# Four FFN layers, four base addresses: moving a kernel's split weights and block sums by 64 to 192 bytes

## The chip, the cores and the metric

The kernel runs on one NeuronCore of a Trainium2 chip, as one program. The metric is device microseconds of that core; lower is better. The time before is 1921.73 us, the median of 3 runs (1921.44 to 1924.72).

## The reference, cut to what matters

Two layers, each a feed-forward network (FFN), a mixer, and another FFN, on 512 tokens of width 1024 in float32. There are four FFNs, and only they matter here:

```
def swiglu(x, w_gate, w_up, w_down):
    return (jax.nn.silu(x @ w_gate) * (x @ w_up)) @ w_down

h = rms_norm(x, ffn1_norm[i])
x = x + 0.5 * swiglu(h, ffn1_w_gate[i], ffn1_w_up[i], ffn1_w_down[i])
# ... a mixer (recurrence, convolution, attention) ...
h = rms_norm(x, ffn2_norm[i])
x = x + 0.5 * swiglu(h, ffn2_w_gate[i], ffn2_w_up[i], ffn2_w_down[i])
```

The hidden width is 2816, that is 22 tiles of 128.

## The kernel before, in words

**Precision.** Every float32 operand is split in two fp32r parts, hi (written by ACT) and lo (the rest, written by DVE). A product is three matmuls on TensorE (PE): hi times hi, lo of the moving operand times hi of the weights, hi of the moving operand times lo of the weights. `product` (lines 797 to 799) and `gu_product` (lines 861 to 863) issue these three. Each matmul has its own load of 128x128 weights, which shows under PEld and runs beside the matmul before it.

**A hidden tile.** Tokens are handled transposed: 128 rows of the width on the partitions, tokens along the free dimension. The first two tiles of each layer are "plain" (`plain_tile`): gate and up, eight blocks of the width, 2 x 8 x 3 = 48 matmuls of 512 columns. The other 20 ("hidden" tiles, `hidden_tile`) use a scheme with seven products in place of eight on halves of the tokens: per product 4 pairs of blocks x 3 = 12 matmuls of 256 columns. The seven weight pieces of a tile (gate, up, and sums of them) lie in `gw_hi` and `gw_lo`. Pieces 0, 1, 5 and 6 are multiplied with `xs_hi`/`xs_lo`, the split input; pieces 2, 3 and 4 with `xu_hi`/`xu_lo`, the split block sums of the input, which are made once a layer. A full tile issues pieces 0, 1, 2, then 6 of the tile before, then 3, 4 and 5: 84 matmuls. All wait on counting semaphores (`gw_lo_done`, `copy_done`, `prod_done`); ACT's next split of a piece (`gw_high`) waits for the product that read the piece before.

**The rest.** After 6, 14 and 22 tiles, down units multiply the hidden activations `a_hi`/`a_lo` with streamed weights `w_hi`/`w_lo`, in matmuls of 512 columns. SP issues the loads of `gu` (the raw gate and up weights) and `raw` in a written-out order; POOL adds two of the sums by DMA. The order on every engine is written by hand.

**Addresses.** `sb` places tiles one after another on every partition, in multiples of 32 bytes, or at a byte that it is told. The bases in the program before are:

| tile | base | base modulo 256 |
|---|---|---|
| xs_hi, xs_lo | 17536, 33920 | 128 |
| w_hi, w_lo | 66688, 74880 | 128 |
| a_hi, a_lo | 83072, 99456 | 128 |
| t0, t1, t2 | 121920 and on | 64 |
| gu | 153280 | 192 |
| gw_hi, gw_lo | 175808, 190144 | 192 |
| xu_hi, xu_lo | 204480, 216768 | 192 |

Every block, piece, pair and token half inside these FFN tiles is a multiple of 512 bytes away from its base, so each FFN matmul reads its moving operand and its weights at these residues.

Of the kernel before, what the change touches and what calls it, by code (L numbers as in the profile page):

```python
# [7 lines left out]
F32 = mybir.dt.float32  # L8
F32R = mybir.dt.float32r
# [5 lines left out]
P = 128  # L15
# [172 lines left out]
def build(nc, xt_in, gu_stream, w_stream, vec_in, bd_in, relb_in, onehot_in, ident_in, out):  # L188
# [3 lines left out]
    with ExitStack() as ctx:  # L192
        top = [(nc.sbuf_base + 31) // 32 * 32]

        def sb(name, shape, dt=F32, at=None):

            size = int(np.prod(shape[1:])) * 4
            if at is None:
                at, top[0] = top[0], top[0] + (size + 31) // 32 * 32
            return nc.alloc_sbuf_tensor_at(name, shape, dt, offset=at)  # L200
# [47 lines left out]
        head_sel = sb("head_sel", [P, 2])  # L248
        stage = top[0]
        gu = sb("gu", [P, 11, PIECE])  # L250
        gw_hi = sb("gw_hi", [P, 7, PIECE], F32R)
        gw_lo = sb("gw_lo", [P, 7, PIECE], F32R)
        xu_hi = sb("xu_hi", [P, PAIRS, 3 * TH], F32R)
        xu_lo = sb("xu_lo", [P, PAIRS, 3 * TH], F32R)
        ffn_top = top[0]

        top[0] = stage
        q_hi = sb("q_hi", [P, 2, T], F32R)
# [310 lines left out]
        def plain_bank(r, which):  # L569
            return (ps_s, ps_t)[r][:, which, :]  # L570
# [223 lines left out]
        def _(pe):  # L794
# [57 lines left out]
                start_unit(n)  # L852
                blocks(s, range(KT), of_x(1), of_x(0)).then_inc(unit_done, 1)

            def gu_product(ps, piece, hi, lo, first, wait=None):

                for j in range(PAIRS):
                    if wait:
                        wait(j)
                    w = slice(j * P, (j + 1) * P)  # L860
                    pe.matmul(ps, gw_hi[:, piece, w], hi(j), start=first and j == 0, stop=False, skip_group_check=True)  # L861
                    pe.matmul(ps, gw_hi[:, piece, w], lo(j), start=False, stop=False, skip_group_check=True)  # L862
                    mm = pe.matmul(ps, gw_lo[:, piece, w], hi(j), start=False, stop=j == PAIRS - 1, skip_group_check=True)  # L863
                mm.then_inc(prod_done, 1)

            def of_u(d, part):
# [1 line left out]
                w = slice(part * TH, (part + 1) * TH)  # L868
                return lambda j: xs_hi[:, 2 * j + d, w], lambda j: xs_lo[:, 2 * j + d, w]

            def of_xu(part):
                w = slice(part * TH, (part + 1) * TH)
                return lambda j: xu_hi[:, j, w], lambda j: xu_lo[:, j, w]

            def square_sum(i):
                pe.wait_ge(const_done, 2)
# [9 lines left out]
            def plain_part(f, j, which, k):  # L886

                piece, w = PLAIN_PIECES[j][2 * (k % 2) + which], slice(k // 2 * P, k // 2 * P + P)
                if k == 0:
                    pe.wait_ge(gw_lo_done, 1 + which if f == 0 else split_count(f, 0))  # L890
                if k == 1:
                    pe.wait_ge(gw_lo_done, split_count(f, 1))
                return product(plain_bank(f % 2, which), gw_hi[:, piece, w], gw_lo[:, piece, w], xs_hi[:, k, :], xs_lo[:, k, :],
                               not plain_started[which], k == KT - 1)

            plain_started = [False, False]
# [34 lines left out]
            def hidden_tile(f, j, i):  # L931

                r, first, more, n = f % 2, j == PLAIN, pended(j), BLOCK_NO[f]
                operands = 4 * FFN_NO[i]

                def landed(sem):
                    return (lambda k: pe.wait_ge(sem, operands + k + 1)) if first else None

                def a12_u2():
                    pe.wait_ge(gw_lo_done, split_count(f, 3))  # L940
                    gu_product(block_bank(r, 0), 5, *of_u(1, 0), True)

                pe.wait_ge(gw_lo_done, split_count(f, 0))
                if n:
                    pe.wait_ge(copy_done, 3 * n)
                gu_product(chain, 0, *of_u(0, 0), True)
                if plain(f - 2):
                    pe.wait_ge(hidden_done, f - 1)
                else:
                    pe.wait_ge(gate_done, 2 * (f - 2) + 1)  # L950
                gu_product(block_bank(r, 2), 1, *of_u(0, 1), True, landed(ua_done))
                pe.wait_ge(gw_lo_done, split_count(f, 1))
                pe.wait_ge(copy_done, 3 * n + 1)
                gu_product(chain, 2, *of_xu(1), False, landed(uc_done))
                if not more:
                    a12_u2()
                elif not plain(f - 1):
                    gate_right(f - 1)
                pe.wait_ge(gw_lo_done, split_count(f, 2))
                if first:  # L960
                    gu_product(block_bank(r, 1), 4, *of_xu(2), False)
                pe.wait_ge(copy_done, 3 * n + 2)
                gu_product(chain, 3, *of_xu(0), False)
                if not first:
                    gu_product(block_bank(r, 1), 4, *of_xu(2), False)
                if more:
                    a12_u2()

            def gate_right(f):

                pe.wait_ge(gw_lo_done, split_count(f, 4))
                pe.wait_ge(up_done, BLOCK_NO[f] + 1)
                gu_product(block_bank(f % 2, 2), 6, *of_u(1, 1), False)

            def down_part(i, u, ks):

# [327 lines left out]
        def _(act):  # L1304
# [48 lines left out]

            def block_x_hi(i, j):
                act.wait_ge(u4_done, PAIRS * FFN_NO[i] + j + 1)
                act.activation(xu_hi[:, j, :].rearrange("p (h t) -> p h t", t=TH), scr[j][:, 3:6, :], ACT.Copy).then_inc(uc_hi_done, 1)

            def right_x_hi(i, j):

# [7 lines left out]
            def plain_high(f, k):  # L1367

                j, r = f % FT, f % 2
                w, src = plain_split(k, j, r)  # L1370
                act.wait_ge(gu_landed[r], landed_count(f))
                if (j, k) == (1, 1):
                    act.wait_ge(prod_done, prod_count(f - 1, "odd"))
                elif f - j:
                    act.wait_ge(prod_done, prod_count(f - j - 1, 3))
                act.activation(gw_hi[:, w, :], src, ACT.Copy, scale=-1.0 if k else 1.0).then_inc(gw_hi_done, 1)

            def norm_std(i):
                act.wait_ge(ssq_done, i + 1)
# [3 lines left out]
            def gw_high(f, k):  # L1383

                r, n = f % 2, BLOCK_NO[f]
                w, src = gu_split(k, r)
                if k == 0:
                    act.wait_ge(gu_landed[r], landed_count(f))
                    act.wait_ge(s1_landed, 16 * (n + 1))
                elif k == 2:  # L1390
                    act.wait_ge(s3_landed, 16 * (n + 1))
                elif k != 3:
                    act.wait_ge(sum_done, 2 * n + (1 if k == 1 else 2))
                if plain(f - 1):
                    act.wait_ge(prod_done, prod_count(f - (2 if k < 2 else 1), "even" if k == 2 else "odd"))
                else:
                    act.wait_ge(prod_done, prod_count(f - 1, (5, 6, 7 if plain(f - 2) else 4, 2, 3)[k]))
                act.activation(gw_hi[:, w, :], src, ACT.Copy).then_inc(gw_hi_done, 1)  # L1398

            def chain_copy(f, p, out):  # L1400
                act.wait_ge(prod_done, prod_count(f, p))
# [429 lines left out]
            act.wait_ge(vec_landed, 16)  # L1831
            act.wait_ge(s1_loaded[0], 16)
            for part in range(2):
                act.activation(gw_hi[:, part, :], gu[:, part, :], ACT.Copy).then_inc(gw_hi_done, 1)
                if part == 0:
                    act.wait_ge(x_landed[0], 16)
                    split_x(0, 0)
# [16 lines left out]
        def _(dve):  # L1854
# [942 lines left out]
```

## Time and profile before

| what | before |
|---|---|
| median of 3 runs | 1921.73 us |
| span of the profiled execution (its own time, first to last instruction) | 1922.5 us |
| PE busy | 1887.3 us (98%) |
| DVE busy | 1462.5 us (76%) |
| ACT busy | 1020.9 us (53%) |
| matmuls | 11902 |

A busy PE in this profile is not a PE at its peak: matmuls overlap, each is shown with a latency, and what one costs is the distance from its start to the start of the next.

### The profile page before, as it was taken

The numbers are of one execution on the slowest core, as the hardware profiler recorded it, in microseconds if no ns is written. First come the engines' busy times: TensorE is split into PE (matmuls) and PEld (weight loads), VectorE is DVE, ScalarE is ACT, GpSimd is POOL, SyncE is SP. The second block draws the span as 40 slices with busy tenths as digits, with TensorE's granted clock in tenths as the row PEclk, the third lists the DMA queues.
The fourth block names the chain that finished last, engine by engine and source line by source line (L and its number), as shares of the span: only waits on it lengthen the run. The fifth ranks groups of instructions, "written<-read, shape, count | busy, mean of one in ns | idle before, by whom it ended". The sixth has DMA issues, their size and how long they took to land.

```text
span 1922.5 us, 31441 instructions
## 1 busy us (share of the span) xinstructions
PE 1887.3 (98%) x11902; PEld 1674.8 (87%) x11902; DVE 1462.5 (76%) x2330; ACT 1020.9 (53%) x1640; POOL 193.0 (10%) x251
## 2 busy tenths in 40 slices
PE   7999999999999999999999999999999999999999
PEld 6899799888878899898889989887778779898997
DVE  8878487667779778597887949756988878687684
ACT  7546154477776455264644626454455766364451
POOL 1311010000001111010110101011111001011010
PEclk9999999999999999999999999999999999999999
DMA  7666862321126655462466646166765376566441
GB/s 240 169 171 182 131 188 61 110 77 57 65 102 173 170 151 152 149 175 97 136 167 165 166 132 181 50 152 161 171 148 133 85 202 171 157 168 168 133 115 66
DMA packets 94662, 271.18 MB, mean 141 GB/s; under 512 B 10568, under 2 KB 10824, under 8 KB 94512
## 3 DMA queue, kind: packets, MB, share of 16 engines
q1 hardware_dynamic: 63456, 201.22, 31.7%
q0 software_dynamic: 29232, 64.50, 19.4%
q10 hardware_dynamic: 1824, 3.44, 1.0%
q8 instruction: 95, 1.56, 0.3%
q14 instruction: 55, 0.45, 0.1%
HBM read 223.07 MB, written 2.28 MB: 117 GB/s over the span
## 4 chain that ended last, share of the span: by engine, by line
PE 85%; DVE 8%; ACT 3%; issue 2%; DMA 1%; ACTq 0%; DVEq 0%
PE ps_unit L797 12%; PE ps_unit L798 12%; PE ps_unit L799 12%; PE ps_y L861 6%; PE ps_y L863 6%; PE ps_y L862 6%; PE ps_s L861 4%; PE ps_s L863 4%; PE ps_s L862 4%; PE ps_t L861 4%; PE ps_t L863 3%; PE ps_t L862 3%; PE ps_s L797 1%; PE ps_s L798 1%; PE ps_s L799 1%
## 5 line engine op out<-in xcount | busy, mean ns | idle before, releaser
L1398 ACT ACTIVATE gw_hi<-gu 128x512 fp32r<-128x512 f32 (+1 forms) x400 | 318.9, 799 | 151.0 <-PE ps_s L863 67.5
L1932 DVE TENSOR_TENSOR gw_lo<-gu,gw_hi 128x512 fp32r<-128x512 f32 (+1 forms) x400 | 354.8, 901 | 49.0 <-ACT gw_hi L1398 36.7
L797 PE MATMUL ps_unit<-a_hi,w_hi 128*128 128x512 f32 x892 | 352.8, 395 | 9.2 <-DVE w_lo L1860 6.5
L798 PE MATMUL ps_unit<-a_lo,w_hi 128*128 128x512 f32 x892 | 349.1, 391 | 0.0
L799 PE MATMUL ps_unit<-a_hi,w_lo 128*128 128x512 f32 x845 | 330.1, 391 | 0.0
L1333 ACT ACTIVATE w_hi<-raw 128x1024 fp32r<-128x1024 f32 (+1 forms) x125 | 125.2, 1003 | 314.0 <-PE ps_unit L799 296.3
L797 PEld LDWEIGHTS ps_unit<-a_hi,w_hi 128*128 128x128 f32 x892 | 168.4, 189 | 48.8 <-DVE w_lo L1860 9.4
L2065 DVE TENSOR_TENSOR t<-ps_unit,half 128x512 f32<-128x512 f32 x96 | 66.4, 691 | 172.4 <-PE ps_unit L799 171.8
L798 PEld LDWEIGHTS ps_unit<-a_lo,w_hi 128*128 128x128 f32 x892 | 168.4, 189 | 33.2
L799 PEld LDWEIGHTS ps_unit<-a_hi,w_lo 128*128 128x128 f32 x845 | 159.5, 189 | 34.1
L861 PE MATMUL ps_y<-xu_hi,gw_hi 128*128 128x256 f32 x640 | 180.3, 282 | 0.3 <-ACT sqb L1402 0.3
L863 PE MATMUL ps_y<-xu_hi,gw_lo 128*128 128x256 f32 x640 | 180.3, 282 | 0.0
L862 PE MATMUL ps_y<-xu_lo,gw_hi 128*128 128x256 f32 x640 | 179.4, 280 | 0.0
L1860 DVE TENSOR_TENSOR w_lo<-raw,w_hi 128x1024 fp32r<-128x1024 f32 (+1 forms) x125 | 143.9, 1152 | 22.9 <-ACT w_hi L1333 22.9
L742 POOL DMA_DIRECT2D gu<-gu_stream_dram x80 | 74.5, 931 | 728.7 <-DMA gu<-gu_stream_dram 722.0
L797 PE MATMUL ps_unit<-xs_hi,w_hi 128*128 128x512 f32 x360 | 145.8, 405 | 0.0
L798 PE MATMUL ps_unit<-xs_lo,w_hi 128*128 128x512 f32 x360 | 140.3, 390 | 0.0
L861 PE MATMUL ps_t<-xs_hi,gw_hi 128*128 128x256 f32 x480 | 134.3, 280 | 2.1 <-DVE t L1994 2.1
L861 PE MATMUL ps_s<-xs_hi,gw_hi 128*128 128x256 f32 x480 | 133.5, 278 | 0.0
L862 PE MATMUL ps_s<-xs_lo,gw_hi 128*128 128x256 f32 x480 | 133.2, 277 | 0.0
L862 PE MATMUL ps_t<-xs_lo,gw_hi 128*128 128x256 f32 x480 | 133.1, 277 | 0.0
L863 PE MATMUL ps_t<-xs_hi,gw_lo 128*128 128x256 f32 x480 | 132.9, 277 | 0.0
(322 smaller groups left out, 4666.9 us busy)
## 6 DMA issues: line engine op xcount, KB each, us to landing
gu<-gu_stream_dram SPq DMA_DIRECT2D x176, 512.0 KB, 5.2
raw<-w_stream_dram SPq DMA_DIRECT2D x136, 512.0 KB, 3.3
gu<-gu_stream_dram SPq DMA_DIRECT2D x80, 256.0 KB, 3.0
gu<-gu_stream_dram POOLq DMA_DIRECT2D x80, 256.0 KB, 4.5
gu<-gu POOLq DMA_DIRECT2D x80, 256.0 KB, 3.3
w_lo<-raw POOLq DMA_DIRECT2D x28, 512.0 KB, 5.1
raw<-w_stream_dram SPq DMA_DIRECT2D x32, 384.0 KB, 3.5
w_lo_3rd<-raw POOLq DMA_DIRECT2D x15, 512.0 KB, 5.2
```

The lines of the kernel that those rows point to most:

```text
L742: pool.dma_start(gu[:, 8 + r, :], gu_stream[f, 1][:, 1, :], accum_op=ALU.add).then_inc(s1_landed, 16)
L797: pe.matmul(ps, lhs_hi, rhs_hi, start=first, stop=False)
L798: pe.matmul(ps, lhs_hi, rhs_lo, start=False, stop=False)
L799: return pe.matmul(ps, lhs_lo, rhs_hi, start=False, stop=last)
L861: pe.matmul(ps, gw_hi[:, piece, w], hi(j), start=first and j == 0, stop=False, skip_group_check=True)
L862: pe.matmul(ps, gw_hi[:, piece, w], lo(j), start=False, stop=False, skip_group_check=True)
L863: mm = pe.matmul(ps, gw_lo[:, piece, w], hi(j), start=False, stop=j == PAIRS - 1, skip_group_check=True)
L1333: act.activation(w_hi[:, s, 0:width(n)], raw[:, slot, 0:width(n)], ACT.Copy).then_inc(w_hi_done, 1)
L1398: act.activation(gw_hi[:, w, :], src, ACT.Copy).then_inc(gw_hi_done, 1)
L1860: dve.tensor_tensor(w_lo[:, s, w], raw[:, slot, w], w_hi[:, s, w].bitcast(F32), ALU.subtract).then_inc(w_lo_done, 1)
L1932: dve.tensor_tensor(gw_lo[:, w, :], src, gw_hi[:, w, :].bitcast(F32), ALU.subtract).then_inc(gw_lo_done, 1)
L2065: dve.tensor_tensor(t0[:, :], ps_unit[:, s, :], half[:, :], ALU.mult).then_inc(unit_read, 1)
```

## The change

In each of the four FFN layers (counted 0 to 3) `gw_hi`, `gw_lo`, `xu_hi` and `xu_lo` become tensors of their own, at bases that are shifted by a number of bytes. All instructions, waits, loads and their order stay. The residues modulo 256 that follow are:

| layer | gw before | gw after | xu before | xu after | xs (not moved) |
|---|---|---|---|---|---|
| 0 | 192 | 192 | 192 | 128 | 128 |
| 1 | 192 | 0 | 192 | 192 | 128 |
| 2 | 192 | 128 | 192 | 192 | 128 |
| 3 | 192 | 64 | 192 | 192 | 128 |

```
+GW_SHIFT = (0, 64, 192, 128)
+XU_SHIFT = (192, 256, 256, 256)
...
-        gw_hi = sb("gw_hi", [P, 7, PIECE], F32R)
-        gw_lo = sb("gw_lo", [P, 7, PIECE], F32R)
-        xu_hi = sb("xu_hi", [P, PAIRS, 3 * TH], F32R)
-        xu_lo = sb("xu_lo", [P, PAIRS, 3 * TH], F32R)
-        ffn_top = top[0]
+        gw_at, xu_at = top[0], top[0] + 2 * 7 * PIECE * 4
+        gw_hi = [sb(f"gw_hi{n}", [P, 7, PIECE], F32R, at=gw_at + GW_SHIFT[n]) for n in range(4)]
+        gw_lo = [sb(f"gw_lo{n}", [P, 7, PIECE], F32R, at=gw_at + GW_SHIFT[n] + 7 * PIECE * 4) for n in range(4)]
+        xu_hi = [sb(f"xu_hi{n}", [P, PAIRS, 3 * TH], F32R, at=xu_at + XU_SHIFT[n]) for n in range(4)]
+        xu_lo = [sb(f"xu_lo{n}", [P, PAIRS, 3 * TH], F32R, at=xu_at + XU_SHIFT[n] + PAIRS * 3 * TH * 4) for n in range(4)]
+        ffn_top = xu_at + max(XU_SHIFT) + 2 * PAIRS * 3 * TH * 4
...
-                    pe.matmul(ps, gw_hi[:, piece, w], hi(j), start=first and j == 0, stop=False, skip_group_check=True)
+                    pe.matmul(ps, gw_hi[f // FT][:, piece, w], hi(j), start=first and j == 0, stop=False, skip_group_check=True)
...
-                return lambda j: xu_hi[:, j, w], lambda j: xu_lo[:, j, w]
+                return lambda j: xu_hi[f // FT][:, j, w], lambda j: xu_lo[f // FT][:, j, w]
```

Every other place that names one of the four tiles takes the layer's own in the same way.

## Rows read from the trace of the kernel before

**Rows 1.** The page: span, busy time of each engine (share, instructions).
```profile
span 1922.5 us, 31441 instructions
...
PE 1887.3 (98%) x11902; PEld 1674.8 (87%) x11902; DVE 1462.5 (76%) x2330; ACT 1020.9 (53%) x1640; POOL 193.0 (10%) x251
```

**Rows 2.** Windows, four tiles each: length; PE, PEld, DVE, ACT, POOL; clock, DMA share, GB/s.
```profile
130.53:169.57 39.04, 39.04 (x338) 39.04 (x337) 35.30 (x49) 24.34 (x42) 6.43 (x8) 1.00 0.72 188
697.89:736.93 39.04, 39.04 (x339) 39.04 (x337) 35.30 (x49) 24.30 (x42) 7.01 (x8) 1.00 0.72 190
1039.54:1078.58 39.04, 39.04 (x339) 39.04 (x338) 35.29 (x49) 24.29 (x42) 6.99 (x8) 1.00 0.74 190
...
1814.75:1853.79 39.04, 39.04 (x339) 39.04 (x337) 35.32 (x49) 24.32 (x42) 6.54 (x8) 1.00 0.74 188
```

**Rows 3.** Timeline of PE in two tiles of layer 0: start, length, matmul.
```profile
150.05 0.28 PE L861 MATMUL ps_y<-xs_hi,gw_hi 128*128 128x256 f32 x1
...
151.41 0.28 PE L861 MATMUL ps_s<-xs_hi,gw_hi 128*128 128x256 f32 x1
...
156.99 0.28 PE L861 MATMUL ps_s<-xu_hi,gw_hi 128*128 128x256 f32 x1
...
158.43 0.29 PE L861 MATMUL ps_s<-xs_hi,gw_hi 128*128 128x256 f32 x1
...
162.53 0.28 PE L861 MATMUL ps_y<-xu_hi,gw_hi 128*128 128x256 f32 x1
```

**Rows 4.** Groups by form, matmuls with gw weights: count, busy us, mean ns.
```profile
L861 PE MATMUL ps_y<-xu_hi,gw_hi 128*128 128x256 f32 x640 | 180.3, 282 | 0.3 <-ACT sqb L1402 0.3
...
L861 PE MATMUL ps_t<-xs_hi,gw_hi 128*128 128x256 f32 x480 | 134.3, 280 | 2.1 <-DVE t L1994 2.1
L861 PE MATMUL ps_s<-xs_hi,gw_hi 128*128 128x256 f32 x480 | 133.5, 278 | 0.0
...
L861 PE MATMUL ps_y<-xs_hi,gw_hi 128*128 128x256 f32 x320 | 88.7, 277 | 0.0
...
L861 PE MATMUL ps_s<-xu_hi,gw_hi 128*128 128x256 f32 x160 | 45.3, 283 | 0.0
...
L861 PE MATMUL ps_t<-xu_hi,gw_hi 128*128 128x256 f32 x160 | 45.3, 283 | 0.0
...
L797 PE MATMUL ps_t<-xs_hi,gw_hi 128*128 128x512 f32 x64 | 27.2, 425 | 0.0
```

**Rows 5.** Timeline of PE: a plain tile of layer 2, then an output unit.
```profile
941.54 0.39 PE L799 MATMUL ps_t<-xs_hi,gw_lo 128*128 128x512 f32 x1
...
943.41 0.39 PE L798 MATMUL ps_t<-xs_lo,gw_hi 128*128 128x512 f32 x1
...
547.64 0.39 PE L797 MATMUL ps_unit<-a_hi,w_hi 128*128 128x512 f32 x1
...
549.90 0.39 PE L798 MATMUL ps_unit<-a_lo,w_hi 128*128 128x512 f32 x1
```

**Rows 6.** Timeline of DVE in the first of those tiles, layer 0.
```profile
159.31 0.69 DVE L1932 TENSOR_TENSOR gw_lo<-gu,gw_hi 128x512 fp32r<-128x512 f32 x1
```

**Rows 7.** Groups by form, whole span: DVE and ACT with other operand addresses.
```profile
L1932 DVE TENSOR_TENSOR gw_lo<-gu,gw_hi 128x512 fp32r<-128x512 f32 x240 | 164.9, 687 | 24.9 <-ACT gw_hi L1398 18.6
...
L1398 ACT ACTIVATE gw_hi<-gu 128x512 fp32r<-128x512 f32 x240 | 151.0, 629 | 107.3 <-PE ps_s L863 42.0 <-DVE gu L1952 35.8 <-PE ps_t L863 29.5
...
L2003 DVE TENSOR_TENSOR a_lo<-t,a_hi 128x512 fp32r<-128x512 f32 x88 | 60.4, 687 | 6.8 <-ACT a_hi L1413 5.6
...
L1413 ACT ACTIVATE a_hi<-t 128x512 fp32r<-128x512 f32 x88 | 55.7, 633 | 9.5 <-DVE t L1999 8.4 <-DVE t L1972 1.0
```

**Rows 8.** Layer 0 around 200 us: timelines of ACT and PE, then a window.
```profile
195.81 7.78 ACTq L1663 DMA_DIRECT2D bias_t<-skew  x16
...
206.06 0.79 PE L797 MATMUL ps_unit<-a_hi,w_hi 128*128 128x512 f32 x1 [3.66 <-DVE w_lo L1860]
...
205.34:212.16 6.82, 6.09 (x14) 4.79 (x15) 3.79 (x5) 0.36 (x1) 0.00 (x0) 0.50 0.89 110
```

More of the change, by code:

```diff
@@ L853, in x_unit, with gu_product @@
                 blocks(s, range(KT), of_x(1), of_x(0)).then_inc(unit_done, 1)
-            def gu_product(ps, piece, hi, lo, first, wait=None):
+            def gu_product(f, ps, piece, hi, lo, first, wait=None):
                 for j in range(PAIRS):
@@ L860, in gu_product @@
                     w = slice(j * P, (j + 1) * P)
-                    pe.matmul(ps, gw_hi[:, piece, w], hi(j), start=first and j == 0, stop=False, skip_group_check=True)
-                    pe.matmul(ps, gw_hi[:, piece, w], lo(j), start=False, stop=False, skip_group_check=True)
-                    mm = pe.matmul(ps, gw_lo[:, piece, w], hi(j), start=False, stop=j == PAIRS - 1, skip_group_check=True)
+                    pe.matmul(ps, gw_hi[f // FT][:, piece, w], hi(j), start=first and j == 0, stop=False, skip_group_check=True)
+                    pe.matmul(ps, gw_hi[f // FT][:, piece, w], lo(j), start=False, stop=False, skip_group_check=True)
+                    mm = pe.matmul(ps, gw_lo[f // FT][:, piece, w], hi(j), start=False, stop=j == PAIRS - 1, skip_group_check=True)
                 mm.then_inc(prod_done, 1)
@@ L869, in of_u, with of_xu @@
                 return lambda j: xs_hi[:, 2 * j + d, w], lambda j: xs_lo[:, 2 * j + d, w]
-            def of_xu(part):
+            def of_xu(f, part):
                 w = slice(part * TH, (part + 1) * TH)
-                return lambda j: xu_hi[:, j, w], lambda j: xu_lo[:, j, w]
+                return lambda j: xu_hi[f // FT][:, j, w], lambda j: xu_lo[f // FT][:, j, w]
             def square_sum(i):
@@ L892, in plain_part @@
                     pe.wait_ge(gw_lo_done, split_count(f, 1))
-                return product(plain_bank(f % 2, which), gw_hi[:, piece, w], gw_lo[:, piece, w], xs_hi[:, k, :], xs_lo[:, k, :],
+                return product(plain_bank(f % 2, which), gw_hi[f // FT][:, piece, w], gw_lo[f // FT][:, piece, w], xs_hi[:, k, :], xs_lo[:, k, :],
                                not plain_started[which], k == KT - 1)
@@ L940, in a12_u2 @@
                     pe.wait_ge(gw_lo_done, split_count(f, 3))
-                    gu_product(block_bank(r, 0), 5, *of_u(1, 0), True)
+                    gu_product(f, block_bank(r, 0), 5, *of_u(1, 0), True)
                 pe.wait_ge(gw_lo_done, split_count(f, 0))
@@ L945, in hidden_tile @@
                     pe.wait_ge(copy_done, 3 * n)
-                gu_product(chain, 0, *of_u(0, 0), True)
+                gu_product(f, chain, 0, *of_u(0, 0), True)
                 if plain(f - 2):
@@ L950, in hidden_tile @@
                     pe.wait_ge(gate_done, 2 * (f - 2) + 1)
-                gu_product(block_bank(r, 2), 1, *of_u(0, 1), True, landed(ua_done))
+                gu_product(f, block_bank(r, 2), 1, *of_u(0, 1), True, landed(ua_done))
                 pe.wait_ge(gw_lo_done, split_count(f, 1))
                 pe.wait_ge(copy_done, 3 * n + 1)
-                gu_product(chain, 2, *of_xu(1), False, landed(uc_done))
+                gu_product(f, chain, 2, *of_xu(f, 1), False, landed(uc_done))
                 if not more:
@@ L960, in hidden_tile @@
                 if first:
-                    gu_product(block_bank(r, 1), 4, *of_xu(2), False)
+                    gu_product(f, block_bank(r, 1), 4, *of_xu(f, 2), False)
                 pe.wait_ge(copy_done, 3 * n + 2)
-                gu_product(chain, 3, *of_xu(0), False)
+                gu_product(f, chain, 3, *of_xu(f, 0), False)
                 if not first:
-                    gu_product(block_bank(r, 1), 4, *of_xu(2), False)
+                    gu_product(f, block_bank(r, 1), 4, *of_xu(f, 2), False)
                 if more:
@@ L972, in gate_right @@
                 pe.wait_ge(up_done, BLOCK_NO[f] + 1)
-                gu_product(block_bank(f % 2, 2), 6, *of_u(1, 1), False)
+                gu_product(f, block_bank(f % 2, 2), 6, *of_u(1, 1), False)
             def down_part(i, u, ks):
@@ L1355, in block_x_hi @@
                 act.wait_ge(u4_done, PAIRS * FFN_NO[i] + j + 1)
-                act.activation(xu_hi[:, j, :].rearrange("p (h t) -> p h t", t=TH), scr[j][:, 3:6, :], ACT.Copy).then_inc(uc_hi_done, 1)
+                act.activation(xu_hi[FFN_NO[i]][:, j, :].rearrange("p (h t) -> p h t", t=TH), scr[j][:, 3:6, :], ACT.Copy).then_inc(uc_hi_done, 1)
             def right_x_hi(i, j):
@@ L1375, in plain_high @@
                     act.wait_ge(prod_done, prod_count(f - j - 1, 3))
-                act.activation(gw_hi[:, w, :], src, ACT.Copy, scale=-1.0 if k else 1.0).then_inc(gw_hi_done, 1)
+                act.activation(gw_hi[f // FT][:, w, :], src, ACT.Copy, scale=-1.0 if k else 1.0).then_inc(gw_hi_done, 1)
             def norm_std(i):
@@ L1397, in gw_high @@
                     act.wait_ge(prod_done, prod_count(f - 1, (5, 6, 7 if plain(f - 2) else 4, 2, 3)[k]))
-                act.activation(gw_hi[:, w, :], src, ACT.Copy).then_inc(gw_hi_done, 1)
+                act.activation(gw_hi[f // FT][:, w, :], src, ACT.Copy).then_inc(gw_hi_done, 1)
             def chain_copy(f, p, out):
@@ L1833, in _ @@
             for part in range(2):
-                act.activation(gw_hi[:, part, :], gu[:, part, :], ACT.Copy).then_inc(gw_hi_done, 1)
+                act.activation(gw_hi[0][:, part, :], gu[:, part, :], ACT.Copy).then_inc(gw_hi_done, 1)
                 if part == 0:
@@ L1894, in block_x_lo @@
                 dve.wait_ge(uc_hi_done, PAIRS * FFN_NO[i] + j + 1)
-                dve.tensor_tensor(xu_lo[:, j, :].rearrange("p (h t) -> p h t", t=TH), scr[j][:, 3:6, :],
-                                  xu_hi[:, j, :].rearrange("p (h t) -> p h t", t=TH).bitcast(F32), ALU.subtract).then_inc(uc_done, 1)
+                dve.tensor_tensor(xu_lo[FFN_NO[i]][:, j, :].rearrange("p (h t) -> p h t", t=TH), scr[j][:, 3:6, :],
+                                  xu_hi[FFN_NO[i]][:, j, :].rearrange("p (h t) -> p h t", t=TH).bitcast(F32), ALU.subtract).then_inc(uc_done, 1)
             def right_x_lo(i, j):
@@ L1931, in gw_low @@
                 dve.wait_ge(gw_hi_done, split_count(f, k))
-                dve.tensor_tensor(gw_lo[:, w, :], src, gw_hi[:, w, :].bitcast(F32), ALU.subtract).then_inc(gw_lo_done, 1)
+                dve.tensor_tensor(gw_lo[f // FT][:, w, :], src, gw_hi[f // FT][:, w, :].bitcast(F32), ALU.subtract).then_inc(gw_lo_done, 1)
             def plain_low(f, k):
@@ L1938, in plain_low @@
                 if k:
-                    dve.scalar_tensor_tensor(gw_lo[:, w, :], src, -1.0, gw_hi[:, w, :].bitcast(F32), ALU.mult, ALU.subtract).then_inc(gw_lo_done, 1)
+                    dve.scalar_tensor_tensor(gw_lo[f // FT][:, w, :], src, -1.0, gw_hi[f // FT][:, w, :].bitcast(F32), ALU.mult, ALU.subtract).then_inc(gw_lo_done, 1)
                 else:
-                    dve.tensor_tensor(gw_lo[:, w, :], src, gw_hi[:, w, :].bitcast(F32), ALU.subtract).then_inc(gw_lo_done, 1)
+                    dve.tensor_tensor(gw_lo[f // FT][:, w, :], src, gw_hi[f // FT][:, w, :].bitcast(F32), ALU.subtract).then_inc(gw_lo_done, 1)
             def second_sum(f):
@@ L2658, in _ @@
                 dve.wait_ge(gw_hi_done, part + 1)
-                dve.tensor_tensor(gw_lo[:, part, :], gu[:, part, :], gw_hi[:, part, :].bitcast(F32), ALU.subtract).then_inc(gw_lo_done, 1)
+                dve.tensor_tensor(gw_lo[0][:, part, :], gu[:, part, :], gw_hi[0][:, part, :].bitcast(F32), ALU.subtract).then_inc(gw_lo_done, 1)
                 if part == 0:
```

## The prediction

> **What bounds the kernel now.** I read the page first: PE is busy for 1887.3 of 1922.5 us, 98%, and DVE, the next, for 76% [rows 1]. Then I cut out steady stretches of each FFN layer. Four hidden tiles take 39.04 us in layer 0 and exactly as long in layers 1, 2 and 3, with PE busy throughout at the full clock and DVE for 35.3 us [rows 2]. So a hidden tile costs 39.04 / 4 = 9.76 us, PE paces it, and it does not depend on what else a layer does. Last I read the starts of single matmuls, because no instruction, wait or transfer is added or removed: only what one matmul costs can change.
>
> There the reader is to see that equal matmuls don't cost the same. Piece 0, moving operand xs, has 12 matmuls of 256 columns from 150.05 to 151.41: 0.1133 us each. Piece 4, moving operand xu, has 12 of the same shape, with weights from the same tile, from 156.99 to 158.43: 0.1200 us each [rows 3]. The lengths tell the same, 277 to 280 ns with xs against 282 or 283 with xu [rows 4]. These two prices make the whole tile: 48 xs matmuls x 0.1133 + 36 xu matmuls x 0.1200 = 5.44 + 4.32 = 9.76 us, the measured period [rows 2]. Nothing is left for waits, and the extra is 0.0067 us for each xu matmul, 36 x 0.0067 = 0.24 us a tile.
>
> **What could make the difference.** I write d for the base of the moving operand minus that of the weights, modulo 256. From the table of bases, xs with gw has d = 192, and xu with gw has d = 0. Matmuls of 512 columns give two more points. In a plain tile (xs with gw, d = 192) eight starts take 943.41 - 941.54 = 1.87 us, 0.2337 each; in an output unit (a with w, d = 0) ten take 549.90 - 547.64 = 2.26 us, 0.226 each [rows 5]. So d = 0 is the slow one at 256 columns and the fast one at 512:
>
> | columns | d = 192 | d = 0 |
> |---|---|---|
> | 256 | 0.1133 us | 0.1200 us |
> | 512 | 0.2337 us | 0.226 us |
>
> In units of 0.0067 us, the difference, these are 17 and 18 units, then 35 and 34. The odd numbers of units stand with d = 192, an odd number of 64 bytes, the even ones with d = 0, an even number. The simplest rule with all four points: a matmul takes at least 17 units (256 columns) or 34 (512), and one more where the parity of d / 64 asks for it. I call it the parity rule. It makes d = 64 behave as 192 and d = 128 as 0. No row shows d = 64 or d = 128 in an FFN matmul, so both prices are open between 0 and 0.0067 us of extra, by the nearest rows.
>
> The Trainium skill speaks against any effect: "SBUF — State Buffer", section "SBUF: two separate sides", gives TensorE two independent read ports, one for the moving operand and one for the weights, and says that TensorE waits for nobody. By that rule the four residues would cost the same and the time would stay. The trace disagrees, with 0.1133 against 0.1200 us [rows 3].
>
> **The change part by part.** Counts first. Each of the three matmuls of a product appears 640 + 160 + 160 = 960 times with xu and 480 + 480 + 320 = 1280 times with xs [rows 4]; over three lines and four layers that is 720 xu and 960 xs matmuls of 256 columns a layer. The plain tiles have 96 of 512 columns a layer (64 in one of six such groups). One unit on all of them is 720 x 0.0067 = 4.8 us, 960 x 0.0067 = 6.4 us and 96 x 0.0067 = 0.64 us.
>
> - Layer 0: xu goes from d = 0 to 128 - 192 = 192, the residues that xs and gw already have in this trace. The price is read, not guessed: minus 4.8 us. xs stays.
> - Layer 1 (gw at 0): xu gets d = 192, minus 4.8 us, with both residues moved by 64. xs gets d = 128: by parity plus 6.4 us, and the plain tiles lose their extra, minus 0.64 us. Sum plus 0.96 us.
> - Layer 2 (gw at 128): xu gets d = 64, by parity minus 4.8 us. xs gets d = 0, the slow distance at 256 columns and the fast one at 512: plus 6.4 minus 0.64 us. Sum plus 0.96 us.
> - Layer 3 (gw at 64): xu gets d = 128, by parity as slow as now. xs gets d = 64, by parity as fast as now. Sum 0.
> - ACT and DVE write and read the moved tiles. DVE takes 687 ns for 128x512 whether all lie at residue 192 or at 64 and 128; ACT takes 629 and 633 ns [rows 7]. I take 0; the bound is 4 ns x 400 splits = 1.6 us of ACT time, which PE's queue covers (next point).
> - Does a faster PE only wait later? DVE needs 35.3 / 4 = 8.8 us a tile [rows 2], and a tile with all matmuls at 0.1133 takes 84 x 0.1133 = 9.52 us, so DVE still fits. Of the splits that PE waits for, the one at 159.31 ends at 160.00 and its product (piece 2 of the next tile) starts at 162.53, 2.5 us later [rows 3, 6]. A gain of 0.24 us a tile lies within that. So tile time goes to the end in full.
> - Layer 0 has one stall, 3.66 us at 202 to 206 us, because ACT issues 16 DMAs for 7.78 us ahead of a weight split, and after it PE runs for 6.8 us at half clock (1.2 GHz) [rows 8]. The issue follows an ACT instruction of the last tile, so the stall moves with PE and eats nothing. Whether the clock falls again is open: 6.8 us at half speed cost 3.4 us, and I keep that as a bound on both sides.
>
> Sum by the parity rule: -4.8 + 0.96 + 0.96 + 0 = -2.9 us. On the profiled execution 1922.5 becomes 1919.6; its span is 0.8 us over the median of the runs, so the median becomes 1918.8 us.
>
> **The rivals.** With x and y for the extra of d = 64 and d = 128 at 256 columns, in units, the sum is: layer 0 -4.8; layer 1 -4.8 + 6.4 y; layer 2 -4.8 + 6.4 - 0.64 + 4.8 x; layer 3 -4.8 + 6.4 x + 4.8 y. Together -13.4 + 11.2 (x + y), and up to 1.3 us less by the plain tiles of layers 1 and 3. Parity is x = 0, y = 1.
>
> - Only equal residues cost (x = y = 0): minus 13.4, 1908.3 us, or 1907.0 with the plain tiles. For it: the one slow case at 256 columns is d = 0. Against it: at 512 columns d = 0 is the fast one, so equality alone doesn't cost.
> - Only d = 192 is a good fit at 256 columns (x = y = 1): the xs products of layers 1 to 3 pay 6.4 us each, only layers 0 and 1 win with xu, plus 9.0 us, 1930.7 us: slower. It decides from x + y = 1.2 on. For it: one good distance is all that the trace shows. Against it: the good distance differs between 256 and 512 columns, so it is no single one.
> - The moving operand's address alone counts (192 slow, 128 fast): only layer 0 wins, minus 4.8 us, 1916.9 us. Against it: 512-column matmuls with moving residue 128 cost 0.226 or 0.2337 us by what the weights' tile is [rows 5].
> - The address is not the cause, something else in xu is: no change, 1921.7 us. Against it: the moving data differ in nothing else that a matmul sees.
>
> **How the numbers follow.** Parity 0.48, equal residues only 0.2, only d = 192 0.1, moving operand alone 0.08, no effect 0.06, values of x and y in between 0.08. The likeliest gives 1918.8 us; its own range is 1915.4 to 1922.2, by the clock's 3.4 us. The range for all is 1906.5 to 1925.0: it takes in equal residues with the plain tiles and leaves out the slow rival. About 0.2%, 3.8 us, is what a measurement of this kernel can tell from no change. Parity's 2.9 us is below that, and I give it 0.1 of its 0.48 above the bound and 0.01 on the slow side. Faster: 0.1 + 0.2 + 0.05 + 0.03 = 0.38. Slower: 0.1 + 0.01 + 0.05 of the mixed and clock cases = 0.16. The same: 0.46.
>
> **What would show it.** In layer 0 four hidden tiles should take 4 x 9.52 = 38.1 us, with xu matmuls 0.1133 us apart; this is the surest step. In layers 1 and 2 four tiles should take 4 x (36 x 0.1133 + 48 x 0.12) = 39.4 us, with the slow matmuls now those of xs and the plain tiles' at 0.227; in layer 3 39.04 as now. If layer 1's xs matmuls stay at 0.1133 us, y is 0 and the time falls under 1915; if layer 3's rise to 0.12, x is 1 and the kernel is slower. The prediction is wrong at its root if xu in layer 0 stays at 0.12.

## The result, and the profile after

The changed kernel takes 1932.02 us (median of 3 runs, 1927.64 to 1932.78), 1.0044 of the time before, with a 95% interval of 1.0031 to 1.0057: slower by 0.44%, where 1918.8 us and most likely "the same" were forecast.

The page of the kernel after, the lines that answer to [rows 1]:

```profile
span 1931.0 us, 31441 instructions
...
PE 1893.5 (98%) x11902; PEld 1682.4 (87%) x11902; DVE 1462.9 (76%) x2330; ACT 1020.7 (53%) x1640; POOL 193.3 (10%) x251
```

The same instructions, DVE and ACT unchanged to 0.4 us, PE 6.2 us busier, the span 8.5 us longer. Where it went, by layer: the timeline of PE, the first FFN matmul of layers 1, 2 and 3, before and then after:

```profile
582.27 0.40 PE L797 MATMUL ps_s<-xs_hi,gw_hi 128*128 128x512 f32 x1
...
923.93 0.40 PE L797 MATMUL ps_s<-xs_hi,gw_hi 128*128 128x512 f32 x1
...
1576.59 0.40 PE L797 MATMUL ps_s<-xs_hi,gw_hi 128*128 128x512 f32 x1
```
```profile
583.04 0.40 PE L800 MATMUL ps_s<-xs_hi,gw_hi 128*128 128x512 f32 x1
...
925.82 0.39 PE L800 MATMUL ps_s<-xs_hi,gw_hi 128*128 128x512 f32 x1
...
1583.05 0.39 PE L800 MATMUL ps_s<-xs_hi,gw_hi 128*128 128x512 f32 x1
```

Four hidden tiles of each layer after, windows with the columns of [rows 2]:

```profile
130.31:169.88 39.57, 39.57 (x338) 39.57 (x337) 35.29 (x49) 24.32 (x42) 6.34 (x9) 1.00 0.72 187
698.97:738.25 39.28, 39.28 (x339) 39.28 (x338) 35.32 (x49) 24.33 (x41) 6.59 (x8) 1.00 0.70 186
1042.10:1082.15 40.05, 40.05 (x339) 40.05 (x337) 35.32 (x49) 24.28 (x42) 6.95 (x8) 1.00 0.71 186
1812.27:1851.95 39.68, 39.68 (x338) 39.68 (x337) 35.15 (x48) 24.39 (x41) 6.16 (x8) 1.00 0.66 175
```

Behind the down groups every layer's tile is longer than the 39.04 / 4 = 9.76 us of [rows 2], with PE at its full clock (1.00) and busy throughout. The differences between layer starts, with the mixers in them, and 1931.0 - 1583.05 for the last, give the account:

| layer | a tile behind the down groups, after | predicted | layer's change, measured | predicted |
|---|---|---|---|---|
| 0 | 9.89 us | 9.52 us | +0.77 us | -4.8 us |
| 1 | 9.82 us | 9.84 us | +1.12 us | +0.96 us |
| 2 | 10.01 us | 9.84 us | +4.57 us | +0.96 us |
| 3 | 9.92 us | 9.76 us | +2.04 us | 0 |

The column measured adds up to the 8.5 us. Layer 0, the step called the surest, is the one most wrong. Its timeline of PE shows why: the end of the tile ahead of the first down group, the products behind it, and the tile of [rows 3]:

```profile
74.51 0.28 PE L864 MATMUL ps_t<-xs_hi,gw_hi 128*128 128x256 f32 x1
...
75.87 0.40 PE L800 MATMUL ps_unit<-a_hi,w_hi 128*128 128x512 f32 x1
...
78.22 0.36 PE L864 MATMUL ps_t<-xs_hi,gw_hi 128*128 128x256 f32 x1 [0.80 <-DVE t L1997]
78.41 0.28 PE L865 MATMUL ps_t<-xs_lo,gw_hi 128*128 128x256 f32 x1
...
79.59 0.28 PE L866 MATMUL ps_t<-xs_hi,gw_lo 128*128 128x256 f32 x1
...
150.10 0.28 PE L864 MATMUL ps_y<-xs_hi,gw_hi 128*128 128x256 f32 x1
...
151.51 0.28 PE L864 MATMUL ps_s<-xs_hi,gw_hi 128*128 128x256 f32 x1
```

Up to 75.87 us twelve matmuls take 1.36 us, 0.1133 each, as in [rows 3]. From 78.41 on ten take 1.18 us, and at 150.10 twelve take 1.41 us: 0.118 us each, with xs and gw at the same addresses as before. So d = 192 has two paces, 0.1133 us (9.52 us a tile) and about 0.1178 us (9.89 / 84). The four tiles ahead of the first down group got the first, the sixteen behind it the second.

The trace of the kernel before has both paces too. Its timeline of PE in layer 0, behind the first down group: the first two xs products, then the third matmul of the xs product that follows the first xu product, and the start of the next product:

```profile
112.25 0.28 PE L861 MATMUL ps_y<-xs_hi,gw_hi 128*128 128x256 f32 x1
...
113.66 0.28 PE L861 MATMUL ps_s<-xs_hi,gw_hi 128*128 128x256 f32 x1
...
116.76 0.28 PE L863 MATMUL ps_s<-xs_hi,gw_lo 128*128 128x256 f32 x1
...
117.89 0.28 PE L861 MATMUL ps_y<-xu_hi,gw_hi 128*128 128x256 f32 x1
```

Right behind the down group twelve xs matmuls take 1.41 us, 0.1178 each; behind the first xu product ten take 1.13 us, 0.113 each. All eight down groups of that trace are followed by this change.

In layer 2 both even and odd distances appear (timeline of PE):

```profile
946.00 0.39 PE L800 MATMUL ps_t<-xs_hi,gw_hi 128*128 128x512 f32 x1
...
947.81 0.39 PE L802 MATMUL ps_t<-xs_hi,gw_lo 128*128 128x512 f32 x1
...
1052.11 0.28 PE L864 MATMUL ps_y<-xs_hi,gw_hi 128*128 128x256 f32 x1
...
1053.55 0.28 PE L864 MATMUL ps_t<-xs_hi,gw_hi 128*128 128x256 f32 x1
...
1059.27 0.28 PE L864 MATMUL ps_t<-xu_hi,gw_hi 128*128 128x256 f32 x1
...
1060.68 0.29 PE L864 MATMUL ps_t<-xs_hi,gw_hi 128*128 128x256 f32 x1
```

xs (d = 0) takes 1.44 / 12 = 0.1200 us, and the plain tile at d = 0 takes 1.81 / 8 = 0.226 us, both as predicted; xu (d = 64) takes 1.41 / 12 = 0.1175 us, where 0.1133 was forecast.

### The profile page after: what moved, and what is told of

Read it like the earlier page. It is cut to its first block, busy times and chain, and to the rows that moved or that the text cites. A ratio compares the mean times of both kernels' runs of the same rounds, so it can differ in the third digit from the quotient of the medians.

```text
span 1931.0 us, 31441 instructions
## 1 busy us (share of the span) xinstructions
PE 1893.5 (98%) x11902; PEld 1682.4 (87%) x11902; DVE 1462.9 (76%) x2330; ACT 1020.7 (53%) x1640; POOL 193.3 (10%) x251
## 3 DMA queue, kind: packets, MB, share of 16 engines
q0 software_dynamic: 29232, 64.50, 19.4%
## 4 chain that ended last, share of the span: by engine, by line
PE 81%; DVE 10%; ACT 3%; issue 3%; DMA 2%; ACTq 0%; DVEq 0%; POOL 0%; POOLq 0%
PE ps_unit L800 12%; PE ps_unit L802 12%; PE ps_unit L801 12%; PE ps_y L864 5%; PE ps_y L866 5%; PE ps_y L865 5%; PE ps_s L866 4%; PE ps_s L864 4%; PE ps_s L865 4%; PE ps_t L864 4%; PE ps_t L866 3%; PE ps_t L865 3%; PE ps_s L800 1%; DMA raw<-w_stream_dram 1%; DVE cv L2456 1%
## 5 line engine op out<-in xcount | busy, mean ns | idle before, releaser
L866 PE MATMUL ps_s<-xs_hi,gw_lo 128*128 128x256 f32 x480 | 135.0, 281 | 0.0
```

The costliest lines, as they stand in the source:

```text
L866: mm = pe.matmul(ps, gw_lo[f // FT][:, piece, w], hi(j), start=False, stop=j == PAIRS - 1, skip_group_check=True)
```

## The experiments

**The theory of two paces:** at an odd distance (64 or 192 bytes) a matmul of 256 columns runs steadily at 0.1133 or at 0.1178 us, and what PE did just before decides which. In the kernel before, the slow xu stretches (d = 0) in every tile brought the xs stretches to the quick pace, so giving xu d = 192 too takes that away. Its rival: d = 192 costs 0.1133 us by itself, and something else in layer 0 costs the rest. Letters in the expectations are those of each expectation.

**d = 192 for both operands in all four layers.** The edit, against the changed kernel:

```
-GW_SHIFT = (0, 64, 192, 128)
-XU_SHIFT = (192, 256, 256, 256)
+GW_SHIFT = (0, 0, 0, 0)
+XU_SHIFT = (192, 192, 192, 192)
```

> gw stays at residue 192 in all four layers and xu goes to 128 in all four, so that every 256-column matmul with gw weights has d = 192. Theory A, memory of the pace: at d = 192 there are two steady paces, 0.1133 and 0.1178 us, and the stretch of matmuls before decides which one a run of equal matmuls falls into and keeps. Each layer then starts at 0.1133 us (hidden tile 9.52 us) and changes to 0.1178 us (9.89 us) at its first down group, as layer 0 of the changed kernel did: about +0.8 us a layer, 1925 us. Rival B, something in layer 0 alone (its start, its transfers) slowed it there: layers 1 to 3 keep 9.52 us, -4.8 us each, about 1908 us.

Measured 1926.27 us, 1.0021 of before (1.0012 to 1.0031). Windows of layer 1, two tiles ahead of the first down group and four behind it:

```profile
612.83:631.87 19.04, 19.04 (x171) 19.04 (x169) 18.13 (x26) 12.80 (x22) 3.50 (x4) 1.00 0.76 196
695.39:734.97 39.58, 39.58 (x339) 39.58 (x337) 35.30 (x49) 24.31 (x42) 6.17 (x8) 1.00 0.71 187
```

9.52 us a tile ahead, 9.89 behind, in all four layers. The rival falls. Here xs and gw lie where they lay before; only xu moved, and the xs products behind the down groups lost their 0.1133 us. Their price depended on their neighbours.

**Other distances.** The edit, against the changed kernel:

```
-GW_SHIFT = (0, 64, 192, 128)
-XU_SHIFT = (192, 256, 256, 256)
+GW_SHIFT = (128, 192, 64, 0)
+XU_SHIFT = (192, 192, 192, 64)
```

> One distance for xs and xu in each of the first three layers: d = 64 in layer 0, d = 0 in layer 1, d = 128 in layer 2; in layer 3 d = 192 for xs and 64 for xu. Theory A with the parity rule for the paces that exist: layer 1 has one pace, 0.1200 us, 10.08 us a tile; layers 0 and 3 have 9.52 us before the first down group and 9.89 us after it; layer 2 about 0.1188 us, as xs of layer 1 in the changed kernel, 9.97 us. The parity rule of the prediction alone: 9.52 us in layers 0 and 3, 10.08 us in layers 1 and 2, throughout.

Measured 1939.08 us, in one run. Windows of layer 1 (d = 0 for both), layer 2 (d = 128 for both: two tiles ahead of the first down group, four behind), layer 3 (xs 192, xu 64: the same two places):

```profile
691.12:731.44 40.32, 40.32 (x338) 40.32 (x337) 35.29 (x48) 24.42 (x41) 6.12 (x7) 1.00 0.64 172
964.06:983.99 19.93, 19.93 (x170) 19.93 (x169) 18.48 (x26) 12.91 (x23) 3.55 (x4) 1.00 0.73 184
1058.26:1098.58 40.32, 40.32 (x338) 40.32 (x337) 35.51 (x49) 24.32 (x41) 6.51 (x8) 1.00 0.70 183
1622.55:1641.93 19.38, 19.38 (x170) 19.38 (x169) 18.45 (x26) 12.93 (x22) 3.52 (x4) 1.00 0.71 190
1695.63:1735.20 39.57, 39.57 (x338) 39.57 (x337) 35.01 (x48) 24.34 (x41) 6.10 (x7) 1.00 0.66 174
```

40.32 / 4 = 10.08 us is 84 x 0.1200: both even distances can cost that all through a tile. Layer 2, forecast at 9.97 throughout, has that ahead of the down group (19.93 / 2) and 10.08 behind it. Layer 3, odd distances only, is at 9.69, where 9.52 was forecast, and then at 9.89. Layer 0 (64 bytes for both) takes 9.52 us for the tile from 66.41 to 75.93 us, ahead of its first down group, and 9.89 behind it. So at 256 columns the even and odd classes are real, and the odd class has the two paces, at 64 bytes as at 192. The paces can also stand side by side: in the tiles of 9.69 us the xs products (192) take 1.36 or 1.37 us and the xu products (64) 1.41.

**Slow matmuls in front of the products, by halving the end of each down group.** The last two blocks of the last down unit of a group are multiplied in halves of 256 columns (12 matmuls at d = 0), once with d = 192 in all layers, once in the kernel before.

```
...
+                pe.matmul(ps, w_hi[:, s, w], hi_x(k)[:, c], start=False, stop=False)
+                pe.matmul(ps, w_hi[:, s, w], lo_x(k)[:, c], start=False, stop=False)
+                mm = pe.matmul(ps, lo[:, w], hi_x(k)[:, c], start=False, stop=last)
...
```

> As e1, and the last two blocks of the last down unit of each group are done in 12 matmuls of 256 columns in place of 6 of 512 (same operands, d = 0, the same sums). Theory A: after 256-column matmuls at d = 0 a d = 192 run falls into the fast pace, as after the xu products of the kernel before; hidden tiles take 9.52 us in all groups, -4.8 us a layer, +0.5 us for the halves, about 1903 us. Rival B, and any theory by which only the addresses of a matmul itself set its cost: within 0.5 us of e1.

> The kernel before with the same halves at the end of each group. Theory A: no change beyond +0.5 us, since each tile's xu products at d = 0 bring the xs products into the fast pace anyway; about 1922 us. A rival by which the halves help of themselves (another wait, a better order): it gains as much as e2 gains on e1.

Measured 1927.86 us (1.0025, 1.0015 to 1.0034) and 1924.54 us (1.0009, 1.0000 to 1.0019). A miss for the first, forecast at about 1903 us: the halves were slow, but the products right behind them stayed at 0.1178, at all eight groups. In the kernel before, the halves gained nothing. Timeline of PE, layer 1, the last halves and the first products, and a window behind them:

```profile
673.92 0.28 PE L995 MATMUL ps_unit<-a_hi,w_hi 128*128 128x256 f32 x1
...
675.35 0.28 PE L865 MATMUL ps_y<-xs_hi,gw_hi 128*128 128x256 f32 x1
```
```profile
693.72:733.29 39.57, 39.57 (x338) 39.57 (x337) 35.29 (x49) 24.30 (x42) 6.12 (x7) 1.00 0.72 187
```

1.43 / 12 = 0.119 us for the halves; 9.89 us a tile. A run of slow matmuls is not enough as such.

Behind one of these eight groups, the second of layer 0, the pace changed later. Timeline of PE at a wait in front of product 2 of the first tile, and a window of four tiles behind it:

```profile
243.74 0.36 PE L865 MATMUL ps_y<-xu_hi,gw_hi 128*128 128x256 f32 x1 [0.29 <-ACT sqb L1426]
```
```profile
250.77:288.85 38.08, 38.08 (x339) 38.08 (x338) 34.97 (x48) 24.33 (x40) 5.27 (x6) 1.00 0.70 187
```

Ahead of this wait of 0.29 us the products run at 0.1178 us, behind it at 0.1133, 9.52 us a tile, for the rest of the group, though no matmul was added there. With d = 192 in all layers and no halves, PE did not wait at this place and stayed at 9.89 us.

**Turns.** A few extra matmuls into the chain's bank just ahead of product 0 of the first hidden tile behind down groups 0 and 1, with d = 192 in all layers; product 0 then starts that sum anew. An offset of 16 elements makes the turn's distance 0.

```
+TURNS = ([(16, 256)] * 1, [(16, 256)] * 2, [(16, 256)] * 4, [(16, 256)] * 9)
...
+                if j > PLAIN and j - 1 in ENDS:
+                    for at, cols in TURNS[f // FT]:
+                        pe.matmul(ps_y[:, 0:cols], gw_hi[f // FT][:, 0, 0:P], xs_hi[:, 0, at:at + cols], start=True, stop=True, skip_group_check=True)
```

> All four layers have the distance 192 bytes for both x operands, as in the run with 192 in all layers, and just before the first gate and up product after down groups 0 and 1 the layers 0, 1, 2 and 3 issue 1, 2, 4 and 9 extra matmuls of 256 columns at distance 0 (their sums land in a bank that is overwritten later). Theory A (a distance-192 product has two steady paces, 0.1133 and 0.1178 us, and the stretch just before decides; a run of slow distance-0 products turns it to the quick one, as each xu stretch did in the kernel before): layer 3 with nine is back at tiles of 9.52 us after each down group instead of 9.89; if one slow product is enough, all layers are, and the kernel takes about 1907 us; with layer 3 alone 1922. Rival B (the quick pace needs slow products in every tile, as the kernel before had): one or two tiles at 9.52 us after each turn, then 9.89, total about 1926. Rival C (what happens before makes no difference, the accumulated work sets it): 9.89 us everywhere after the first group, 1928.

> The same with other turns: layer 0 one extra matmul of 128 columns at distance 192, layer 1 one of 64 columns at distance 192, layers 2 and 3 three and six of 256 columns at distance 0. Theory A: layer 3 (six) goes to tiles of 9.52 us after its down groups, layer 2 lies between one and four of the other run; the short products of layers 0 and 1 only shift the phase: if a phase is what is remembered, one of them turns its layer to 9.52 us as well, else both stay at 9.89. If only layer 3 turns, about 1922 us; if all do, about 1907. Rival C (nothing before makes a difference): 9.89 us everywhere after the first group, 1927.

> As the kernel with 192 in all layers and one turn each, of 256, 192, 32 and 128 columns in layers 0 to 3, all at distance 192. If it is the moment at which a product starts against something periodic that is remembered, a turn of 256 columns, which is one more matmul like those behind it, leaves its layer at 9.89 us after the down groups, and the widths that turn their layer are a matter of length; if any break turns it, all four layers go to 9.52 (about 1905 us). With only the lengths 32 and 128 turning, about 1916.

Measured, one run each: 1915.43, 1908.15 and 1911.29 us (before beside the first two: 1922.01, one run; beside the third: 1922.81). What a tile behind the turn takes:

| turn, per group | layer | tile |
|---|---|---|
| none | all | 9.89 us |
| one of 256 columns, d = 192 | 0 | 9.89 us |
| one of 192 columns, d = 192 | 1 | 9.52 us |
| one of 128 columns, d = 192 | 0 and, in another run, 3 | 9.52 us, in layer 0 behind the first group alone |
| one of 64 columns, d = 192 | 1 | 9.52 us |
| one of 32 columns, d = 192 | 2 | 9.52 us |
| one of 256 columns, d = 0 | 0 | 9.52 us |
| two of 256 columns, d = 0 | 1 | 9.89 us |
| three, four, six, nine, d = 0 | 2, 2, 3, 3 | 9.52 us |

Behind the second group of layer 0 the turn of 128 columns brought the quick pace as well, up to a wait of 0.24 us at 240.06 us; behind that wait the tiles took 9.89 us.

Windows of four tiles: two at d = 0 (layer 1) and nine (layer 3), then 256 columns (layer 0) and 32 columns (layer 2) at d = 192:

```profile
692.73:732.30 39.57, 39.57 (x338) 39.57 (x337) 35.29 (x49) 24.31 (x42) 6.31 (x8) 1.00 0.70 187
1685.67:1723.76 38.09, 38.09 (x339) 38.09 (x338) 35.15 (x49) 24.34 (x41) 7.04 (x8) 1.00 0.75 195
```
```profile
130.03:169.60 39.57, 39.57 (x339) 39.57 (x337) 35.29 (x49) 24.33 (x42) 7.16 (x9) 1.00 0.71 188
1033.58:1071.66 38.08, 38.08 (x338) 38.08 (x337) 35.21 (x49) 24.29 (x41) 6.74 (x8) 1.00 0.75 191
```

One extra matmul changes the price of the next several hundred, so the pace is a state that persists, and neither lengths nor addresses of the products set it alone. One more matmul like those behind it changes nothing, so it is not the extra work or the bank. The rival that slow products are needed in every tile falls.

**The version that gains: 64 columns in every layer, at d = 192 and at the changed kernel's own addresses.**

```
+TURNS = ([(0, 64)],) * 4
```

> Distance 192 bytes for both x operands in all four layers, and one extra matmul of 64 columns before the first gate and up product after down groups 0 and 1 in every layer. Theory A (two paces at distance 192, the stretch before decides): the 64 hidden tiles behind down groups take 9.52 us instead of 9.89, so 64 times 0.37 = 23.7 us less than the run with 192 in all layers (1926.3), plus some 0.1 to 0.2 us for each of the eight turns: 1903 to 1907 us, ratio to the kernel before 0.990 to 0.993. Rival B (the quick pace in the runs with turns came from their slow products or their lengths, not from the break): the tiles stay at 9.89 and the time at 1926.

> The addresses of the changed kernel, untouched, with the same turn of 64 columns in every layer. Theory A: layer 0 (192 for both operands) gets the tiles that the prediction priced, 9.52 us instead of 9.89 behind both down groups, 16 times 0.37 = 5.9 us; in layers 1 to 3 at least one operand has another distance, and a break lasts only until the next stretch of it: 0 to 2 us. In all 1924 to 1928 us, against 1932.0 without the turn. Rival B: no tile changes, 1932 to 1933.

With d = 192 everywhere: 1908.33 us (1903.59 to 1908.79), 0.9923 of before (0.9910 to 0.9935), 0.8% faster; 1903 to 1907 us were forecast. With the changed kernel's addresses: 1926.66 us, 1.0020 of before (1.0011 to 1.0029), against 1.0044 without the turn. Windows of the first, layer 1, and layer 0 behind its second group, and the timeline of PE where that one lost its pace:

```profile
694.23:732.31 38.08, 38.08 (x339) 38.08 (x337) 35.21 (x49) 24.29 (x41) 6.68 (x8) 1.00 0.72 188
257.89:297.46 39.57, 39.57 (x338) 39.57 (x337) 35.30 (x49) 24.28 (x42) 6.38 (x8) 1.00 0.71 186
```
```profile
241.02 0.28 PE L867 MATMUL ps_s<-xs_hi,gw_lo 128*128 128x256 f32 x1
242.27 0.36 PE L865 MATMUL ps_y<-xu_hi,gw_hi 128*128 128x256 f32 x1 [0.98 <-ACT sqb L1409]
```

Behind the wait of 0.98 us layer 0 runs at 9.89 us a tile: 8 x 0.37 = 3.0 us that the mechanism could still give. The other seven groups run at 9.52 us. Against d = 192 without turns PE was busy for 19.4 us less (1887.0 to 1867.6), and the span fell by 17.0 us (1924.0 to 1907.0): 2.4 us went into longer waits. Windows of the second kernel, layers 0, 2 and 3:

```profile
130.80:168.88 38.08, 38.08 (x339) 38.08 (x337) 35.21 (x49) 24.35 (x41) 6.43 (x8) 1.00 0.74 193
1037.25:1077.30 40.05, 40.05 (x338) 40.05 (x337) 35.31 (x49) 24.29 (x42) 7.02 (x9) 1.00 0.71 186
1694.00:1733.68 39.68, 39.68 (x339) 39.68 (x337) 35.20 (x49) 24.30 (x42) 6.25 (x8) 1.00 0.70 184
```

Layer 0, at the changed kernel's very addresses, gets the 38.08 us that the prediction priced (38.1); layers 1 to 3, where even and odd distances alternate, keep their tiles (layer 1 9.82 us; layers 2 and 3 the 40.05 and 39.68 above).

**A second turn, in front of product 2.** It was meant to give that wait's loss back. The turn starts a sum in the bank where product 0's lies, so the gate and up values of the six tiles concerned are changed; only its time is read.

```
+SECOND = ([(0, 64)], [(0, 64)], [(0, 128)], [])
...
+                        pe.matmul(ps_y[:, TH:TH + cols], gw_hi[f // FT][:, 2, 0:P], xs_hi[:, 0, at:at + cols], start=True, stop=True, skip_group_check=True)
```

> The kernel with 192 in all layers and 64-column turns, with a second turn in the first hidden tile after each down group, in front of product 2 and behind the wait there: 64 columns in layers 0 and 1, 128 in layer 2, none in layer 3. Theory A (two paces, what stands before decides; in layer 0 TensorE waited 0.5 us in front of product 2 behind the second down group, and the product behind that wait came out slow and stayed so): the second turn gives layer 0 its 9.52 us back for the seven or eight tiles behind the wait, 2.6 to 3 us, 1905 to 1906 us against 1908.3; in layers 1 and 2 a break put into a quick stretch shows whether a break turns in both directions: if it does, these two layers go to 9.89, 32 tiles by 0.37 = 11.8 us, 1917. Rival B (the wait has nothing to do with it; it is something of layer 0's second group): layer 0 stays at 9.89 there.

Measured 1920.58 us, 0.9990 (0.9981 to 0.9999); 1905 to 1906 us were forecast if the turn acts one way only, 1917 if it also ends a quick stretch. Timeline of PE in layer 0 around both turns, then windows of layers 1 and 3:

```profile
111.93 0.19 PE L953 MATMUL ps_y<-xs_hi,gw_hi 128*128 128x64 f32 x1
...
113.41 0.28 PE L866 MATMUL ps_s<-xs_hi,gw_hi 128*128 128x256 f32 x1
...
114.77 0.19 PE L964 MATMUL ps_y<-xs_hi,gw_hi 128*128 128x64 f32 x1
114.80 0.36 PE L866 MATMUL ps_y<-xu_hi,gw_hi 128*128 128x256 f32 x1
115.00 0.28 PE L867 MATMUL ps_y<-xu_lo,gw_hi 128*128 128x256 f32 x1
...
116.17 0.28 PE L868 MATMUL ps_y<-xu_hi,gw_lo 128*128 128x256 f32 x1
```
```profile
697.92:737.50 39.58, 39.58 (x339) 39.58 (x337) 35.30 (x49) 24.31 (x42) 6.53 (x8) 1.00 0.71 186
1694.16:1732.24 38.08, 38.08 (x339) 38.08 (x337) 35.15 (x49) 24.31 (x41) 7.04 (x8) 1.00 0.72 184
```

Between the turns twelve matmuls take 114.77 - 113.41 = 1.36 us; behind the second turn ten take 116.17 - 115.00 = 1.17 us, 0.117 each. The same 64 columns that bring the quick pace behind a down group end it inside a quick stretch, in layers 0 and 1 behind both groups, and 128 columns do so in layer 2; layer 3, without a second turn, stays at 9.52. A turn acts in both directions. The wait that it was aimed at did not recur in this run. The other traces show that the pace can change at a wait, in both directions, with no turn at that place: from slow to quick at 0.29 us (the halves), from quick to slow at 0.24 and 0.98 us (turns in layer 0). It need not: at 0.36 us (one 256-column turn at d = 0, layer 0) it stayed quick, at 0.48 us (the changed kernel, layer 0) slow. What decides it at a wait no run shows.

## Why the prediction was wrong

- **What bounds it** held: PE is busy throughout every window of four tiles, at the full clock, and only the distances of the matmul starts differ. That "tile time goes to the end in full" did not hold where the quick tiles came: the four ahead of layer 0's first down group saved 0.96 us (37.88 to 76.74 before, 37.97 to 75.87 after), and the wait in front of the product behind them grew from 0.22 to 0.80 us.
- **"The price is read, not guessed: minus 4.8 us" (layer 0)** is the step that failed. The row showed 0.1133 us for xs at d = 192 in a tile where slow xu stretches stood between; it was taken as the price of d = 192. It is one of two prices, and the trace of the kernel before held the other, 0.1178 us, behind each down group until the first xu product. The first experiment, in which xu alone moved and xs lost the lower price, shows the same from the other side: without the slow stretches nothing ended the slow pace, and the sixteen tiles behind the down groups kept it. Measured +0.77 us, 5.6 us of the 11.4 us by which the predicted span of 1919.6 us was short. That it was the pace and not the address is shown by the turn: same addresses, 38.08 us.
- **The parity rule** held for the classes at 256 columns: 0.1200 us for d = 0, about 0.1186 to 0.1200 for d = 128 (9.97 and 10.08 us a tile). At 512 columns it held for d = 0 alone (0.226 us): the first 48 plain matmuls of layer 1 (d = 128) take 11.15 us after, 0.232 each, where 0.227 was forecast, and those of layer 3 (d = 64) 10.99 us, 0.229. Its other half, that an odd distance costs 17 units, is wrong for 64 as for 192 bytes: 0.1175 us for xu in layer 2, which missed by 3.6 us, and 9.92 us a tile with xs at 64 in layer 3, which missed by 2.0 us.
- **Layer 1** came out near its number, +1.12 for +0.96 us, in part by luck: the xs products of a tile (d = 128) cost 5.70 us where 5.76 was forecast, xu 4.12 where 4.08 was, and of the 0.64 us that the plain tiles were to give back less than 0.1 came.
- **The check of the two prices by the sum of a tile** was luck in part. In the tile of [rows 3] the two products read, 1.36 and 1.44 us, are the ends of the scale: the four xs products take 1.36, 1.36, 1.38 and 1.38 us, the three xu products 1.42, 1.42 and 1.44. That makes 5.48 + 4.28 = 9.76 as well as 5.44 + 4.32; the first matmuls of the xs product at 158.43 us, right behind an xu product, stand 0.12 us apart and its later ones 0.113, so already there the price depended on the neighbours.
- **The rivals.** The slow one (only d = 192 is good at 256 columns) gives 1930.7 us, close to the result, but by another way: it let layer 0 win 4.8 us, and layer 0 lost. No rival had a price that depends on what stands before a matmul. The rivals by which the address is not the cause, or the moving operand's alone, fall: xs never moved, and its products changed price with the weights' address in layer 2.
- **The rule of the Trainium skill** weighed there ("SBUF — State Buffer", section "SBUF: two separate sides": TensorE waits for nobody) gives no change; the trace disagrees once more, with 9.76, 9.82, 9.89, 9.92 and 10.01 us for the same tile. Whether a read port is what the matmuls wait for no run shows.

What is left open: what in the chip holds the pace, what decides it at a wait, why one, three, four, six and nine slow matmuls turn it and two, or a dozen halves, do not, and what decides it where even and odd distances alternate.

## What to carry to other kernels

A duration read in a trace is the price of an instruction between its neighbours; before it is used elsewhere, look whether the same instruction at the same address has another price in another stretch. Where PE runs back to back and equal matmuls differ by a few per cent, compare the starts of one product over the whole layer, not of one tile: here the other price stood in the same trace, 38 us ahead of the row that was read. An odd distance of moving operand and weights (64 or 192 bytes modulo 256) was never slower here than an even one for 256 columns, but worth its full 5.6% only with the quick pace behind each down group; at 512 columns d = 0 was the quicker one, 0.226 against 0.2337 us.

## What was unexpected of the hardware

- At an odd distance a 256-column matmul has two steady paces, 0.1133 and about 0.1178 us, and each lasts over hundreds of matmuls: 9.52 or 9.89 us a tile.
- One extra matmul of 32 to 192 columns, at d = 192, ahead of the first product behind a down group takes 0.37 us off every tile behind it, up to a wait that turns it back; one of 256 columns at that distance does nothing. Twelve matmuls with a turn of 64 columns in front take 1.48 us, where they take 1.41 without it.
- Put into a quick stretch, the same matmul brings the slow pace.
- A wait of 0.24 to 0.98 us of PE can change the pace in either direction, and then for the rest of the group.
